# Two hybrid layers reordered: convolution columns first, delta-net operands during the projection, attention units between the matmuls of the inverse's levels

## The chip, the cores and the metric

One core of one Trainium2 chip runs the kernel; the time is device microseconds, before the change 1755.29 us in the median of three runs (1745.7 to 1759.51). All work is float32. A matrix product of the projections is made as three matmuls of the numbers' high and low halves, the others as float32 matmuls, which the trace records as two instructions each.

## What is computed

Two hybrid layers, then two layers of another kind, which the change leaves alone. 256 tokens, width 1024. A hybrid layer projects the normalised input, runs three mixers on the columns and projects their joined outputs back; a gated feed-forward block follows.

```python
h = rms_norm(x, norm_mix) * (1 + sc_m) + sh_m
(aq, ak, av, bq, bkc, bvc, bks, bvs, bkw, bvw, bg, cqkv, cz, ca, cb) = jnp.split(h @ w_in, points, axis=-1)
o_a = banded_attention(apply_rope(aq), apply_rope(ak), av, A_WINDOW, attn_sinks)
o_b = nsa_mixer(bq, bkc, bvc, bks, bvs, bkw, bvw, bg, ...)   # compressed, selected, windowed: three gated softmaxes
o_c = gated_delta_net(cqkv, ca, cb, cz, conv_w, A_log, dt_bias, gdn_norm)
x = x + gt_m * (jnp.concatenate([o_a, o_b, o_c], axis=-1) @ w_out)
```

The third mixer:

```python
q, k, v = split(silu(short_causal_conv(cqkv, conv_w)))       # width 4, one channel at a time
q = l2norm(q) * dk ** -0.5; k = l2norm(k)
beta = sigmoid(b); g = -exp(A_log) * softplus(a + dt_bias)
decay = exp(gc_i - gc_j) for j <= i                          # gc: running sum of g in a chunk
a_mat = strictly lower part of (k beta) k^T * decay
u, w = solve (I + a_mat) [v beta, k beta exp(gc)]            # the inverse
```

then a scan over the chunks with the state, and a gated norm with `silu(cz)`. `mod = silu(c) @ ada_w + ada_b` gives the shifts, scales and gates; its matrix is as wide as six widths, and its chunks of 512 columns are spread over the layer.

## The kernel before: how a hybrid layer is staged

Five engines run programs of their own, in order, tied by semaphores. Constants: `P` 128, `S` 256, `CH` 512, `SLOTS` 3, `AHEAD` 3, `LEVELS` 7, `DEPTH` 3.

**Weights.** SP loads chunks of 512 columns (2 MB) into `ring`, which has three slots: the load of chunk n waits for the end of chunk n-3 (`load`), which is the last matmul of a projection chunk, or for an `ada` chunk ACT's copy of its sums (`acc_ready`). Each chunk is two halves. For each half ACT makes the high part (`high`, L1253; three buffers, so a half waits for the use of the half three before it), DVE the low part (`low`, L1676), and PE runs the 48 matmuls of a half (`three`, L623 to L625). ACT issues `high(u+3)` after it has taken the two tiles of half u out of PSUM (`take`, L1270), in its program order: what stands behind a `high` on ACT waits for that chunk's DMA too. The same holds for DVE and `low`.

**Order of chunks in a hybrid layer.** Five column chunks: two for the attention inputs (`raw` tiles 0 to 7, of which 0 to 5 get the rotary embedding), three for the convolution (12 tiles); then `cz`; then `w_tok` (276 columns, 1.1 MB: values, gates, a, b). An `ada` chunk stands behind the third and the fifth.

**Input stage.** PE runs the chunks; `rotate(j)` puts the rotation matmul of a raw tile (L971) between column tiles, and DVE's three operations of it (L1965 to L1967) come back to PE as `rope_done`. DVE runs the convolution: per group of four tiles four operations of the first tap (L1995) and twelve of the others (L1997); ACT the silu (L1385).

**Preparation.** `token_major` (L785): 24 transposes to token-major form, copied by ACT (L1306); `log_decays` (L799, L801); the compression MLP (L1006, L1015, L1022, L1024).

**Attention.** Eight units a layer (two of mixer A, three for each query half of mixer B), with keys of width 128, 256, 15, 128, 128, 15, 256, 256. A unit is a chain over four engines: `scores` on PE (L738), `logits` on DVE (bias and maximum, L1705, L1708), `exps` on ACT (L1276), `recip` on DVE (L1721, L1724), the multiplication on POOL (L2192), `transposes` on PE (L748), `copy_pt` on ACT (L1287), `values` on PE (L761), at the end of an output `evac` on DVE (L1733). Scores alternate between banks 0 and 1 and banks 2 and 3, transposes use 4 and 5, so three units are in flight. DVE makes the delta-net operands in seven steps between units (L1805 to L1828).

**Delta net.** Seven `group`s of four transposes (L785), the products of keys (L820), their masks, and then seven levels of the inverse: T1 (L836, eight products of 128x128), ACT copies them (L1351), two updates (L844, L846), DVE subtracts them (L1858, L1860), POOL masks the matrix for the next level (L2232). PE issues `ada_dots` and `modulations` in levels 1 and 3. Then the tail: U and w, the state, the outputs, the gated norm, two groups of transposes; then the output projection.

`attention` and `delta_net` follow each other in all programs: the first level starts when the last unit is done.

Of the kernel before, what the change touches and what calls it, by code (L numbers as in the profile page):

```python
# [6 lines left out]
ALU = mybir.AluOpType  # L7
# [4 lines left out]
P = 128  # L12
# [31 lines left out]
KQ_BANKS = (4, 5, 6, 3)  # L44
# [16 lines left out]
CN_FIRST, V1_FIRST = 162, 64  # L61
# [20 lines left out]
def hybrid_then_mixture(nc, xT, c, vec1, vec2, consts, dist, table, ada, w_mix, w_tok, w_cmp, w_out, w_gu, w_dn,  # L82
# [46 lines left out]
    IN_ADA = (2, 4)  # L129
# [22 lines left out]

    def ada_bank(m):

        i = m % ADA_L
        return i + 2 if i < ADA_FIRST else 2 if i == ADA_FIRST + 2 else 6
# [12 lines left out]
    with ctx:  # L169
# [79 lines left out]
        tok = view(6656, 3, NCH, GD)  # L249
# [3 lines left out]
        Dm = view(10240, NCH, P)  # L253
        MT = view(21056, NCH, P)
        QKT = view(1024, NCH, P)
        MbT = view(13312, 2, NCH, P)
        X = view(15360, NCH, P)
# [66 lines left out]
        rows_ready = sem("rows_ready")  # L324
        mod_ready = sem("mod_ready")
# [84 lines left out]
        def stage(name, us, woven=False):  # L410

            stages[name] = (len(units), len(units) + len(us))
            for i, U in enumerate(us):
# [3 lines left out]
                U["bank"] = 2 if woven else 2 * ((len(units) + i) % 2)  # L417
# [80 lines left out]
        def _(sp):  # L498
# [35 lines left out]
            for l in range(L1):  # L534
# [11 lines left out]
                for j, at in enumerate(phases[f"in{l}"]["at"]):  # L546
# [5 lines left out]
                    if j in IN_ADA:  # L552
                        load_ada(m + IN_ADA.index(j))
                load(phases[f"tok{l}"]["n0"], w_tok[l], KT * TOKW)
                load_phase(f"cmp{l}", w_cmp[l], 0, full)
# [38 lines left out]
        def _(pe):  # L594
# [4 lines left out]
            def tile_free(name, j):  # L599

                t0 = phases[name]["t0"]
                if name.startswith("tok"):
# [64 lines left out]
            def columns_chunk(name, nn, j, src, ready=None, after=None):  # L667

                for part in range(2):
# [7 lines left out]
                    for m in range(2):  # L677
                        t = j + 2 * part + m
                        tile_free(name, t)
                        channel_tile(bank[:, t % 4, 0:S], w, m * P, src).then_inc(gemm_ready, 1)  # L680
                        if after:
                            after(t)

            def tokens_chunk(name, nn, j):

                for part in range(2):
# [3 lines left out]
                    for qt in range(QT):  # L690
                        if part == 0:
                            tile_free(name, j + qt)
                        last = token_tile(bank[:, (j + qt) % 4, CH // 2 * part:CH // 2 * (part + 1)], w, 0, CH // 2,
# [13 lines left out]
            def ada_dots(m):  # L707
# [3 lines left out]
                for k in range(KT):  # L711
                    rows = slice(32 * (k % 4), 32 * (k % 4) + 32)
                    last = nc.tensor.matmul(bank[rows, ada_bank(m), :], c_wide[:, k, :], w[:, k, :],
                                            start=k < 4, stop=k >= 4, tile_position=(0, 32 * (k % 4)))
                last.then_inc(rows_ready, 1)
# [1666 lines left out]
```

## Time and profile before

| | us |
|---|---|
| median of three runs | 1755.29 |
| the profiled execution, its own time | 1758.94 |
| its span, first to last instruction | 1757.1 |
| PE busy in the span | 1564.1 (89%) |
| DVE / ACT / POOL busy | 1031.5 / 785.3 / 273.1 |
| mean granted clock of PE | 0.934 |
| layer 0, first matmul of the input to first of the output projection | 43.1 to 273.2 |
| layer 1, the same | 534.5 to 758.0 |

Columns of a view of stretches: busy microseconds of an engine and its count of instructions, then the granted PE clock (1.00 is 2.4 GHz, 0.50 is 1.2 GHz), the DMA share and GB/s. In the chain of waits a row has start, length and what the time went into. "Idle before" in square brackets is what an instruction's engine waited for.

### The profile page before, as it was taken

The numbers are of one execution on the slowest core, as the hardware profiler recorded it, in microseconds if no ns is written. First come the engines' busy times: TensorE is split into PE (matmuls) and PEld (weight loads), VectorE is DVE, ScalarE is ACT, GpSimd is POOL, SyncE is SP. The second block draws the span as 40 slices with busy tenths as digits, with TensorE's granted clock in tenths as the row PEclk, the third lists the DMA queues.
The fourth block names the chain that finished last, engine by engine and source line by source line (L and its number), as shares of the span: only waits on it lengthen the run. The fifth ranks groups of instructions, "written<-read, shape, count | busy, mean of one in ns | idle before, by whom it ended". The sixth has DMA issues, their size and how long they took to land.

```text
span 1757.1 us, 29189 instructions
## 1 busy us (share of the span) xinstructions
PE 1564.1 (89%) x12266; PEld 1470.0 (84%) x12266; DVE 1031.5 (59%) x1324; ACT 785.3 (45%) x1178; POOL 273.1 (16%) x102
## 2 busy tenths in 40 slices
PE   5899798989898986989999899569999999999997
PEld 2886487989898864879999799448999988889997
DVE  1575536795664765367554533685876454478743
ACT  3335423434234354334533444354664355556642
POOL 0000255570530002554000000220000001100000
PEclk8997798999999988999999899679999999999999
DMA  8358324554453470244445734203553543245442
GB/s 362 145 218 314 122 97 165 205 205 176 180 195 144 180 285 41 97 152 157 176 156 180 258 144 158 96 1 101 187 191 133 198 172 133 98 154 175 161 151 88
DMA packets 30190, 287.82 MB, mean 164 GB/s; under 512 B 2887, under 2 KB 11367, under 8 KB 11784
## 3 DMA queue, kind: packets, MB, share of 16 engines
q1 hardware_dynamic: 28888, 269.51, 41.9%
q0 software_dynamic: 1152, 16.78, 2.4%
q8 instruction: 79, 1.29, 0.3%
q14 instruction: 23, 0.19, 0.0%
q10 hardware_dynamic: 48, 0.05, 0.0%
HBM read 285.23 MB, written 7.39 MB: 167 GB/s over the span
## 4 chain that ended last, share of the span: by engine, by line
PE 72%; DVE 16%; ACT 4%; issue 4%; DMA 3%; POOL 1%; SPq 0%; DVEq 0%; ACTq 0%
PE bank L623 20%; PE bank L624 19%; PE bank L625 19%; DVE w_lo L1676 4%; DMA ring<-w_mix 3%; PE bank L703 2%; DVE arena L1997 2%; ACT w_hi L1253 1%; PE bank L846 1%; PE bank L748 1%; PE bank L836 1%; DVE h L2118 1%; PE bank L844 1%; PE bank L738 1%; PE bank L761 1%
## 5 line engine op out<-in xcount | busy, mean ns | idle before, releaser
L623 PE MATMUL bank<-hi_T,w_hi 128*128 128x256 f32 x2248 | 653.3, 291 | 41.3 <-DVE h_lo L1659 16.4
L1676 DVE TENSOR_TENSOR w_lo<-ring,w_hi 128x2048 fp32r<-128x2048 f32 (+2 forms) x218 | 515.2, 2373 | 229.7 <-ACT w_hi L1253 228.0
L625 PE MATMUL bank<-hi_T,w_lo 128*128 128x256 f32 x2248 | 647.3, 288 | 0.0
L624 PE MATMUL bank<-h_lo,w_hi 128*128 128x256 f32 x2056 | 592.0, 288 | 0.0
L1253 ACT ACTIVATE w_hi<-ring 128x2048 fp32r<-128x2048 f32 (+3 forms) x226 | 391.8, 1735 | 349.6 <-PE bank L625 278.5
L623 PEld LDWEIGHTS bank<-hi_T,w_hi 128*128 128x128 f32 x2248 | 444.1, 198 | 47.7 <-issue 34.8
L625 PEld LDWEIGHTS bank<-hi_T,w_lo 128*128 128x128 f32 x2248 | 443.7, 197 | 0.0
L624 PEld LDWEIGHTS bank<-h_lo,w_hi 128*128 128x128 f32 x2056 | 405.8, 197 | 0.3
L623 PE MATMUL bank<-act_hi,w_hi 128*128 128x256 f32 x704 | 201.3, 286 | 11.7 <-DVE act_lo L1695 9.9
L624 PE MATMUL bank<-act_lo,w_hi 128*128 128x256 f32 x704 | 200.4, 285 | 0.0
L625 PE MATMUL bank<-act_hi,w_lo 128*128 128x256 f32 x704 | 200.3, 284 | 0.0
L623 PEld LDWEIGHTS bank<-act_hi,w_hi 128*128 128x128 f32 x704 | 135.8, 193 | 12.5 <-DVE act_lo L1695 10.5
L624 PEld LDWEIGHTS bank<-act_lo,w_hi 128*128 128x128 f32 x704 | 135.8, 193 | 0.0
L625 PEld LDWEIGHTS bank<-act_hi,w_lo 128*128 128x128 f32 x704 | 135.7, 193 | 0.0
L1270 ACT ACTIVATE arena<-bank 128x256 f32<-128x256 f32 (+3 forms) x99 | 39.1, 405 | 151.1 <-PE bank L625 151.1
L2155 DVE SCALAR_TENSOR_TENSOR arena<-bank,v,arena 128x254 f32<-128x254 f32 (+1 forms) x176 | 72.7, 475 | 37.2 <-ACT arena L1612 37.0
L2192 POOL TENSOR_TENSOR lg<-lg,rec 128x512 f32<-128x512 f32 (+2 forms) x24 | 31.2, 1301 | 398.8 <-DVE rec L1721 366.0
L2203 POOL TENSOR_TENSOR w_lo<-ring,w_hi 128x2048 fp32r<-128x2048 f32 x8 | 36.0, 4523 | 299.1 <-ACT w_hi L1253 299.1
L2212 POOL TENSOR_TENSOR arena<-arena 128x2048 f32<-128x2048 f32 (+1 forms) x16 | 80.0, 4999 | 1.3
L623 PE MATMUL bank<-w_hi,hi_T 128*128 128x256 f32 (+2 forms) x240 | 68.4, 285 | 8.7 <-DVE w_lo L1676 7.2
L624 PE MATMUL bank<-mix_lo,w_hi 128*128 128x256 f32 x256 | 74.5, 291 | 0.0
L2210 POOL TENSOR_TENSOR arena<-arena,c_silu 128x4096 f32<-128x4096 f32 x8 | 59.4, 7424 | 72.0 <-DMA arena<-ada 72.0
(234 smaller groups left out, 2014.6 us busy)
## 6 DMA issues: line engine op xcount, KB each, us to landing
ring<-w_gu SPq DMA_DIRECT2D x22, 2048.0 KB, 8.4
ring<-w_dn SPq DMA_DIRECT2D x32, 1408.0 KB, 6.0
ring<-w_up SPq DMA_DIRECT2D x22, 2048.0 KB, 8.1
ring<-ada SPq DMA_DIRECT2D x16, 2048.0 KB, 8.2
ring<-w_mix SPq DMA_DIRECT2D x12, 2048.0 KB, 8.2
arena<-ada POOLq DMA_DIRECT2D x8, 2048.0 KB, 9.5
ring<-even_in SPq DMA_DIRECT2D x8, 2048.0 KB, 8.3
ring<-odd_in SPq DMA_DIRECT2D x6, 2048.0 KB, 8.3
```

The costliest lines, as they stand in the source:

```text
L623: nc.tensor.matmul(out, wh, xh, start=start, stop=False)
L624: nc.tensor.matmul(out, wh, xl, start=False, stop=False)
L625: return nc.tensor.matmul(out, wl, xh, start=False, stop=stop)
L703: last = nc.tensor.matmul(bank[:, 7, 0:S], const("ones"), h[:, k, :], start=(k == 0), stop=(k == KT - 1))
L1253: nc.scalar.activation(w_hi[:, u % AHEAD, 0:size], ring[:, slot, part * size:(part + 1) * size], ACT.Copy)\
L1270: nc.scalar.activation(dst, src, func).then_inc(gemm_freed, 1)
L1676: V.tensor_tensor(w_lo[:, n % SLOTS, at], ring[:, n % SLOTS, at], w_hi[:, u % AHEAD, 0:size].bitcast(F32), ALU.subtract).then_inc(w_lo_rea ...
L1997: ins = V.scalar_tensor_tensor(out=conv[:, t, :], in0=src, scalar=wt, in1=conv[:, t, :], op0=ALU.mult, op1=ALU.add)
L2155: V.scalar_tensor_tensor(out=cv[:, b, half, shift:S], in0=bank[:, 2 * b + half, 0:S - shift], scalar=cw[:, tap, at], in1=cv[:, b, half, sh ...
L2203: G.tensor_tensor(w_lo[:, n % SLOTS, at], ring[:, n % SLOTS, at], w_hi[:, u % AHEAD, 0:size].bitcast(F32), ALU.subtract).then_inc(w_lo_rea ...
L2210: ch(G.tensor_tensor(ada_late, ada_late, along(c_silu, CH), ALU.mult))
L2212: ch(G.tensor_tensor(ada_late[:, 0:half], ada_late[:, 0:half], ada_late[:, half:2 * half], ALU.add))
```

## The change

The order of the chunks: the three convolution chunks (`conv{l}`), an `ada` chunk, `w_tok`, the two chunks of raw tiles, an `ada` chunk, `cz` (`in{l}`). The host packs the columns in that order.

In the input stage: ACT takes a convolution tile twice, once as it is and once scaled by the first tap, so DVE's first-tap operations go (12 a layer). The transposes to token-major form are issued between the chunks (`token_major(l, part)`), ACT takes the squared norms of q and k (16 activations with a sum) and scales v by beta (8) straight from PSUM, `log_decays` goes before `cz`, and all operands of the delta net (`unit_rows`, `decayed`) are made by DVE before the mixers start. `rotate` is now issued by hand for two tiles at a time, and waits for DVE's `rope_done` two tiles back.

In the mixers: `attention` and `delta_net` become one `mixing`. Scores and transposes of a unit both use banks 4 and 5 (`bank` 4); so `scores(u)` waits for `logits(u-1)` and for `copy_pt(u-2)`, and `transposes(u)` waits for `logits(u+1)`, the last scores that were issued. In level lv PE issues T1, an `ada` chunk's modulations and the first half of its dots (levels 1 to 5 and 1 to 4), the transposes of unit lv, the updates, the values of unit lv, the other half of the dots, the scores of unit lv+2. Unit 7 stands in the tail. `MbT` and `X` lie in `h` and `mix`; `ada` dots are made in halves of 256 columns through bank 7. ACT's high halves for the output projection move to levels 5 and 6 and the tail, POOL's low halves behind unit 7.

```diff
-        phase(f"in{l}", ["columns"] * 5 + ["tokens"], ada_after=IN_ADA)
+        phase(f"conv{l}", ["columns"] * 3, ada_after=(2,))
         phase(f"tok{l}", ["rows"], KT * TOKW // 2)
+        phase(f"in{l}", ["columns"] * 2 + ["tokens"], ada_after=(1,))
```

PE, in `scores`, then the input stage and the levels:

```diff
+                elif U["bank"] == 4:
...
+                    if u:
+                        pe.wait_ge(logits_done, u)
+                    if u - first >= 2:
+                        pe.wait_ge(pt_ready, u - 1)
...
+            def input_columns(l, ready):
+                columns_chunk(conv_name, 0, 0, src, ready)
+                columns_chunk(conv_name, 1, 4, src)
+                columns_chunk(conv_name, 2, 8, src, parts=(0,))
...
+                token_major(l, 0)
+                columns_chunk(conv_name, 2, 8, src, parts=(1,))
+                ada_dots(m)
...
+                token_major(l, 1)
+                columns_chunk(name, 0, 0, src, first_bank=2, parts=(0,))
+                modulations(m, m + 1)
+                token_major(l, 2)
+                columns_chunk(name, 0, 0, src, first_bank=2, parts=(1,))
+                rotate(l, 0)
+                rotate(l, 1)
+                columns_chunk(name, 1, 4, src, first_bank=2, parts=(0,))
+                rotate(l, 2)
+                rotate(l, 3)
+                columns_chunk(name, 1, 4, src, first_bank=2, parts=(1,))
+                ada_dots(m + 1)
+                log_decays(l)
+                tokens_chunk(name, 2, 8, 2, parts=(0,))
+                rotate(l, 4)
+                rotate(l, 5)
+                tokens_chunk(name, 2, 8, 2, parts=(1,))
+                modulations(m + 1, m + 2)
...
                 for lv in range(LEVELS):
-                    if lv == 3:
-                        modulations(m_next, m_next + 1)
                     pe.wait_ge(mb_ready, l * LEVELS + lv + 1)
-                    if lv in (1, 3):
-                        ada_dots(m_next + lv // 2)
...
                         last.then_inc(t1_ready, 1)
+                    if 2 <= lv <= 5:
+                        modulations(m + lv, m + lv + 1)
+                    if 1 <= lv <= 4:
+                        half_dots(m + 1 + lv, 0)
+                    transposes(u0 + lv)
...
                         last.then_inc(dx_ready, 1)
+                    if lv == 0:
+                        pe.wait_ge(kc_ready, l + 1)
+                    values(u0 + lv)
+                    if 1 <= lv <= 4:
+                        half_dots(m + 1 + lv, 1)
+                    if lv + 2 < len(range(*stages[f"hybrid{l}"])):
+                        scores(u0 + lv + 2)
```

ACT, in the input stage, and DVE, at the end of a level:

```diff
+                conv_silu(l, 0)
+                conv_half(4)
+                rows_of(l, 0)
+                conv_half(5)
+                conv_silu(l, 1)
+                ada_rows(m)
+                high(u0 + 6 + AHEAD)
...
+                high(u0 + 7 + AHEAD)
+                rows_of(l, 1)
+                conv_silu(l, 2)
+                raw_half(0)
...
+                    recip(u0 + lv + 1)
+                    evac(u0 + lv)
+                    if lv + 2 < len(range(*stages[f"hybrid{l}"])):
+                        logits(u0 + lv + 2)
```

The order of the loads on SP's queue, from the second chunk of layer 0's projection, before:

```order
L506 DMA ring<-w_mix 128x4096 x2
L506 DMA ring<-ada 128x4096
L506 DMA ring<-w_mix 128x4096 x2
L506 DMA ring<-ada 128x4096
L506 DMA ring<-w_mix 128x4096
L506 DMA ring<-w_tok 128x2208
L506 DMA ring<-w_cmp 128x4096 x2
L506 DMA ring<-ada 128x4096 x4
```

and now:

```order
L511 DMA ring<-w_mix 128x4096 x2
L511 DMA ring<-ada 128x4096
L511 DMA ring<-w_tok 128x2208
L511 DMA ring<-w_mix 128x4096 x2
L511 DMA ring<-ada 128x4096
L511 DMA ring<-w_mix 128x4096
L511 DMA ring<-w_cmp 128x4096 x2
L511 DMA ring<-ada 128x4096 x4
```

The half-sized `w_tok` now stands behind the first `ada` chunk, and only it lies between that and the next full chunk.

ACT's program behind the take of the last two convolution tiles, now (L1308 is `high`, L1522 the silu, L1320 `ada_rows`, L1384 and L1386 `rows_of`, L1333 `take`):

```order
L1308 ACTIVATE w_hi<-ring 128x2048
L1522 ACTIVATE arena<-arena 128x1024
L1320 ACTIVATE arena<-bank 128x512
L1308 ACTIVATE w_hi<-ring 128x2048
L1333 ACTIVATE arena<-bank 128x276 x2
L1423 ACT_TABLE_LOAD
L1423 ACTIVATE small<-arena 128x12
L1424 ACTIVATE small<-arena 128x4
```

and the stretch of before with the second silu and the first `w_tok` halves (L1253 is `high`, L1385 the silu, L1265 `ada_rows`, L1270 `take`):

```order
L1270 ACTIVATE arena<-bank 128x256 x2
L1253 ACTIVATE w_hi<-ring 128x1104
L1265 ACTIVATE arena<-bank 128x512
L1385 ACTIVATE arena<-arena 128x1024
L1253 ACTIVATE w_hi<-ring 128x1104
L1270 ACTIVATE arena<-bank 128x512 x2
```

Before, nothing that PE needs stood behind the silu's `high`; now the silu that PE's transposes wait for, and the copy of the `ada` sums that frees a ring slot, stand behind the `high` of a chunk that was loaded late.

ACT in levels 1 to 3, before (L1351 copies T1, L1265 `ada_rows`):

```order
L1351 ACTIVATE arena<-bank 128x512 x2
L1265 ACTIVATE arena<-bank 128x512
L1351 ACTIVATE arena<-bank 128x512 x4
L1265 ACTIVATE arena<-bank 128x512
L1351 ACTIVATE arena<-bank 128x512 x6
```

and now, from level 1 on (L1481 copies T1, L1327 is an `ada` half, L1350 `copy_pt`, L1339 `exps`):

```order
L1481 ACTIVATE arena<-bank 128x512 x2
L1327 ACTIVATE arena<-bank 128x256
L1350 ACTIVATE pT<-bank 128x512 x2
L1327 ACTIVATE arena<-bank 128x256
L1339 ACTIVATE lg,sums<-lg,negm 128x15 x4
L1481 ACTIVATE arena<-bank 128x512 x2
L1327 ACTIVATE arena<-bank 128x256
L1350 ACTIVATE pT<-bank 15x512
L1327 ACTIVATE arena<-bank 128x256
```

The exponentials of the next unit stand behind the second half of the `ada` dots, which PE makes at the end of a level.

## Rows read from the trace of the kernel before

**Rows 1.** The page: the chain that ended last, share of the span by engine

```profile
PE 72%; DVE 16%; ACT 4%; issue 4%; DMA 3%; POOL 1%; SPq 0%; DVEq 0%; ACTq 0%
```

**Rows 2.** Stretches: layer 0 whole, its attention; then layer 1 stage by stage

```profile
43.10:273.20 230.10, 197.01 (x1470) 169.50 (x1470) 124.81 (x230) 96.39 (x203) 38.10 (x20) 0.88 0.47 172
158.40:203.50 45.10, 35.01 (x189) 21.64 (x189) 26.91 (x50) 23.22 (x85) 12.67 (x11) 0.61 0.73 250
534.40:630.80 96.40, 88.36 (x685) 84.17 (x686) 58.91 (x101) 35.43 (x48) 0.00 (x0) 0.95 0.44 165
630.80:648.40 17.60, 15.09 (x149) 10.66 (x148) 9.99 (x28) 9.69 (x22) 0.00 (x0) 0.90 0.85 323
648.40:689.60 41.20, 28.85 (x189) 16.84 (x188) 27.10 (x50) 23.65 (x85) 12.68 (x11) 0.75 0.30 118
689.60:701.20 11.60, 8.66 (x45) 7.69 (x45) 5.47 (x10) 4.82 (x9) 0.00 (x1) 0.85 0.00 1
701.20:742.50 41.30, 38.59 (x328) 34.56 (x328) 16.73 (x26) 13.60 (x17) 19.82 (x8) 1.00 0.29 103
742.50:758.00 15.50, 9.94 (x80) 9.09 (x80) 4.59 (x14) 7.41 (x25) 5.60 (x2) 1.00 0.00 1
```

**Rows 3.** The chain that ended last, layer 1 (start, us, what)

```profile
534.47 0.55 PE bank L623
560.14 7.68 DMA ring<-w_mix
567.84 1.92 ACT w_hi L1253
...
605.60 2.20 DVE w_lo L1676
630.51 1.28 ACT L1439
...
732.64 1.16 PE bank L836 x8
738.75 1.16 PE bank L836 x8
758.05 0.38 PE bank L623
```

**Rows 4.** SP's issues of loads in layer 1, in order of time

```profile
548.62 0.33 SPq L506 DMA_DIRECT2D ring<-ada  x1
...
578.41 0.33 SPq L506 DMA_DIRECT2D ring<-w_mix  x1
```

**Rows 5.** DMA issues: KB each, median us to landing

```profile
bias_wide<-bias_dram SPq DMA_DIRECT2D x1, 6144.0 KB, 33.2
ring<-w_tok SPq DMA_DIRECT2D x2, 1104.0 KB, 5.0
```

**Rows 6.** The stretch behind a wait of 3.75 us in layer 1's input stage

```profile
574.00:578.00 4.00, 4.00 (x24) 4.00 (x23) 3.81 (x5) 0.00 (x0) 0.00 (x0) 0.58 0.00 0
```

**Rows 7.** Groups by form in layer 1's mixing and input (busy us, mean ns)

```profile
L2203 POOL TENSOR_TENSOR w_lo<-ring,w_hi 128x2048 fp32r<-128x2048 f32 x3 | 13.5, 4518 | 0.0
L2192 POOL TENSOR_TENSOR lg<-lg,rec 128x1024 f32<-128x1024 f32 x3 | 6.1, 2019 | 5.7 <-DVE rec L1724 3.8 <-DVE rec L1721 1.8
L1276 ACT ACTIVATE lg<-lg,negm 128x256 f32<-128x256 f32 x12 | 5.9, 497 | 0.9 <-DVE negm L1708 0.7 <-DVE esink L1713 0.2
L1705 DVE SCALAR_TENSOR_TENSOR lg<-bank,cn 128x1024 f32<-128x1024 f32 x3 | 3.7, 1224 | 1.5 <-PE bank L738 1.5
L1385 ACT ACTIVATE arena<-arena 128x1024 f32<-128x1024 f32 x3 | 3.2, 1053 | 3.0 <-DVE arena L1997 3.0
```

**Rows 8.** PE in attention at full clock: eight transposes

```profile
658.90 1.10 PE L748 MATMUL bank<-cn,lg 128*128 128x128 f32 x8 [0.17 <-POOL lg L2192]
```

**Rows 9.** DVE and POOL in order of time, layer 0's attention

```profile
191.12 1.52 DVE L1724 TENSOR_TENSOR rec<-rec,small 128x4 f32<-128x4 f32 x1
190.36 4.26 POOL L2192 TENSOR_TENSOR lg<-lg,rec 128x1024 f32<-128x1024 f32 x2 [3.78 <-DVE rec L1724]
```

More of the change, by code:

```diff
@@ L59 @@
 CNW = 2782
-CN_FIRST, V1_FIRST = 162, 64
+CN_FIRST, V1_FIRST = 162, 112
 class Chain:
@@ L665, in token_tile, with columns_chunk @@
                 return last
-            def columns_chunk(name, nn, j, src, ready=None, after=None):
-                for part in range(2):
+            def columns_chunk(name, nn, j, src, ready=None, first_bank=0, parts=(0, 1)):
+                for part in parts:
                     u = phases[name]["u0"] + 2 * nn + part
@@ L679, in columns_chunk, with tokens_chunk @@
                         tile_free(name, t)
[L680 to L686, printed above, removed]
+                        channel_tile(bank[:, (first_bank + t) % 4, 0:S], w, m * P, src).then_inc(gemm_ready, 1)
+            def tokens_chunk(name, nn, j, first_bank=0, parts=(0, 1)):
+                for part in parts:
                     u = phases[name]["u0"] + 2 * nn + part
@@ new lines, in mixing @@
+            def mixing(l):
+                m = ADA_L * l + ADA_FIRST
+                u0 = stages[f"hybrid{l}"][0]
+                pe.wait_ge(xpe_ready, 2 * (l + 1))
+                for kv in range(2):
+                    nn = phases[f"cmp{l}"]["n0"] + kv
+                    chunk_in(nn)
+                    w = ring[:, nn % SLOTS, :].rearrange("p (k n) -> p k n", k=CMP_PAIRS)
+                    for k in range(CMP_PAIRS):
+                        rows = slice(32 * (k % 4), 32 * (k % 4) + 32)
+                        last = nc.tensor.matmul(bank[rows, 6, S * kv:S * kv + S], xpe[:, kv, k, :], w[:, k, :],
+                                                start=k < 4, stop=k >= CMP_PAIRS - 4, tile_position=(0, 32 * (k % 4)))
+                    last.then_inc(gemm_ready, 1)
+                pe.wait_ge(rope_done, 7 * (l + 1))
+                scores(u0)
+                pe.wait_ge(gemm_freed, phases[f"out{l}"]["t0"])
@@ new lines, in blocks @@
+            def blocks(l):
+                ch(V.memset(xpe[:, :, :, :], 0.0))
+                dve.wait_ge(gemm_freed, phases[f"in{l}"]["t0"] + 8)
+                for kv, pe_name in enumerate(("pe_k", "pe_v")):
+                    for two, rows in enumerate((LO, HI)):
+                        base = raw[rows, 6 + kv, :].rearrange("p (n q a) -> p a q n", q=8, a=2)[:, two]
+                        for hf in range(2):
+                            last = V.tensor_tensor(
+                                xpe[rows, kv, 8 * hf:8 * hf + 8, 0:N_CMP], base[:, :, hf:hf + N_CMP],
+                                along(vec(l, pe_name)[rows, 8 * hf:8 * hf + 8], N_CMP), ALU.add)
+                    last.then_inc(xpe_ready, 1)
@@ L2006, in _ @@
-                dve.wait_ge(gate_exp, l + 1)
-                ch(V.tensor_scalar(small[:, 0:32], small[:, 0:32], 1.0, None, ALU.add))
-                ch(V.reciprocal(small[:, 0:32], small[:, 0:32]))
-                softplus(l)
-                decays(l)
-                attention(f"hybrid{l}", operands(l))
-                delta_net(l)
+                input_columns(l)
+                mixing(l)
                 dve.wait_ge(mod_ready, m + 6)
```

625 lines of the change are left out of this document (327 added, 298 removed).

## Prediction

> **What bounds the kernel now.** I read the page's chain first: 72% of it is PE, 16% DVE [rows 1]. Then the stretches of the two layers that are touched. A hybrid layer takes 230.1 us in layer 0 and 223.6 (534.4 to 758.0) in layer 1 [rows 2]; the remaining 1303 us of the span have no changed instruction. In layer 1 PE is busy 88.4 of 96.4 us in the input stage and 38.6 of 41.3 in the levels, at clocks 0.95 and 1.00. In attention it is busy 28.9 of 41.2 at clock 0.75, in layer 0 35.0 of 45.1 at 0.61, so even the busy part is stretched [rows 2]. The time to win is there: a unit is a chain over four engines, and no dense work of PE lies beside it. The chain of waits and SP's issues give the input stage's pace: chunks end at 548.62, 560.14 and 578.41 [rows 3, 4].
>
> **Input stage, layer 1, clock zero at its first matmul (534.47 [rows 3]).** A full chunk takes 560.14-548.62 = 11.5 us, a half 5.8; the first chunk 14.15 (clock) [rows 3, 4]. A load lands after 7.7 us [rows 3], `w_tok` after 5.0 [rows 5]; then ACT's high half 1.9, DVE's low half 2.2 [rows 3]; a table load 1.28 [rows 3], a silu 1.05 [rows 7]. The new order puts these in series four times:
> - `w_tok` may load when chunk 2 ends, 25.7; landed 30.7; its `high` (1.1, half the size) stands ahead of the first silu on ACT: silu done 34.1. PE is done with the half ahead of the transposes at 31.5. **Idle 2.6.**
> - The first raw chunk loads at the end of the third chunk, 40.8, landed 48.5. ACT's `high` 50.3, then silu 2 at 51.4. PE had `ada` dots (1.9) and `w_tok` (6.2), done 48.9. **Idle 2.5.** Transposes, then raw half 1 from 52.5 to 58.3.
> - The second raw chunk waits for the copy of the `ada` sums, behind that silu: 52.0, landed 59.7. ACT stands at its `high` until 61.6, then norms of eight tiles (3.1, from 0.25 to 0.6 each), table and silu: 67.1. PE was ready at 59.2. **Idle 7.9.**
> - `cz` loads at the end of the first raw chunk, 75.5, landed 83.2, high 85.0, low 87.2. DVE's `low` stands ahead of the first rotary tile, for which PE waits from 82.2 until 88.4, and 1.2 for the next. **Idle 7.4.**
>
> A wait of 3.75 us was followed by clock 0.58 for 4 us [rows 6], where 4.0 us of matmuls did the work of 2.3: I add 1.7 behind each of the two long ones, 3.4. PE's own work: before 88.4 busy, of which some 1.5 was such slow clock, so 86.9; plus 24 transposes at 1.10/8 = 0.14 [rows 8], 3, and `log_decays` 1.9. That is 91.8. Sum 91.8+2.6+2.5+7.9+7.4+3.4 = 115.6 against 96.4: **+19**. DVE's 12 first taps (0.3 each) and ACT's 12 added takes lie beside PE and change nothing; ACT's waits are loads, not work. The price is the series of load, high, silu, and with two of three slots behind an `ada` chunk and `w_tok` PE has only 8 us of work to cover a load's 12.
>
> **Mixing, layer 1.** Before, from 630.8 to 758.0: 127.2 us. PE's work in it at full clock: each stretch's busy time by its clock, 15.1 x 0.90 + 28.9 x 0.75 + 8.7 x 0.85 + 38.6 + 9.9 = 91.2 [rows 2]; less the 4.9 that moved to the input: 86.3. What of the rest stays:
> - the key products wait for copies, the masks for the products: 11.6-8.7 = 2.9 stays [rows 2];
> - the tail is a chain of small steps: 15.5-9.9 = 5.6 stays [rows 2];
> - in a level, a unit's steps: with width 256 logits 2 x 1.22+0.3 = 2.7, exps 4 x 0.5 = 2.0, POOL 2.0 [rows 7], `recip` 0.35, copy 1.1: 8.2 off PE. PE has in a level the 5.4 of T1 and updates (of a period of 738.75-732.64 = 6.1 [rows 3]), the dots 1.9, modulations 0.8 and 2 to 3 of the unit: 10 to 11 in levels 1 to 4. That covers the 8.2. It doesn't where the shared banks make `transposes(u)` wait for `logits(u+1)`: level 0 (1.3), level 1 (0.5), levels 5 and 6 without dots (1.4 and 1.1). Sum 4.3.
>
> 86.3+2.9+5.6+4.3 = 99. This takes full clock for all; the levels had it with 93% busy [rows 2]. So layer 1: 115.6+99 = 214.6 against 223.6, **-9**. Scaling a whole stretch by its mean clock overstates the work, since the slow part of the stretch is where the busy rows are: eight transposes took 1.10 at full clock [rows 8], and counted piece by piece attention is 19 and not 21.7, the small pieces of the other stretches about 2 less. I take 95 for the mixing: layer 1 at 210.6, **-13**.
>
> **Layer 0** does the same work: 210.6, plus one thing of its own. The 6 MB `bias_wide` transfer takes 33.2 us [rows 5]; it is issued behind the fourth `ada` load, which now waits for level 1, near 189 us, so it ends near 223, and the first output chunk lands near 228 behind it. ACT's `high` for it stands in level 5, near 225: 2 to 3 us. 213 against 230.1: **-17**.
>
> Late parts: POOL's three low halves (4.5 each [rows 7]) now start in the tail, 14 us before the output projection; the first is needed at its start and the others 5.8 and 11.6 later: hidden, 4 if the tail were 10 shorter. The feed-forward stage starts as before.
>
> **Sum**: 1758.94-30 = 1729 for the profiled execution's own time. The median shown is 3.65 below that time, so 1755.3-30 = 1725; since two of the three bounds I chose (full clock in the mixing, no wait inside levels 2 to 4) are on the good side I take **1728**.
>
> **Bounds.** If the four series of the input stage were fully hidden, the input would be 92+2 and the gain 2 x 20 larger: 1688. If the clock falls in the mixing as in attention before (0.75 for a third of it), 8 a layer are lost: 1744.
>
> **Rivals.**
> 1. *The loads are hidden after all* (another engine's order lets ACT pass): for it, only 8 of 96 us were idle before [rows 2], with three slots too; against it, the silus stand behind the `high` in ACT's program. 1690.
> 2. *DVE and POOL hold each other up.* A `recip` product of 128x4 took 1.52 us instead of 0.16, beginning while POOL's 2.3 us multiplication ran and ending with it [rows 9]. In the levels POOL has 2.0 of mask and up to 2.0 of unit in each, and DVE's small product stands on the way to the next unit. My order of events has POOL done before DVE's product in each level; if it is wrong in each, 2.0 x 7 x 2 = 28 come back: 1756, no change. The Trainium skill (SBUF — State Buffer, "Who interferes with whom") says that a VectorE operation with two SBUF inputs and a GpSimd operation that reads SBUF exclude each other for the whole instruction; by that rule, which those two rows agree with, it depends only on which starts first.
> 3. *The units serialise: slower.* Banks 4 and 5 serve scores and transposes of all units, so fewer are in flight. A unit alone is 8.2 off PE plus 2.9 on it, 11 for width 256 (three), some 6.3 for 128 (three), 4.6 for 15 (two): 61 us. If nothing of it lies beside the 41.3 of the levels, that pair costs 102 where I count about 64: +38 a layer, 1804. It decides from 15 us of uncovered chain a layer on. For it: ACT's `exps` stand behind the second half of the dots, so each unit's chain starts at a level's end. Against: a level of 10 us is longer than the 8.2. Half of it gives 1766, all 1804: I name 1785.
>
> **How the numbers follow.** A measurement of this kernel tells 1% (17.6 us) from no change. The forecast's own case, 1710 to 1737, has 0.5; rival 1 0.12; rival 2 and a fallen clock, 1738 to 1772, 0.26; rival 3 0.12. Faster by over 1% (under 1737.7): 0.62; within 1% 0.26; slower 0.12. Leaving out half of rival 1 and rival 3 gives a range of 1696 to 1763.
>
> **What would show it.** In the changed trace: the input stage to `cz`'s last matmul at 115 us from its start, with PE idle twice for over 6 us, ended by ACT's silu and DVE's rope tile; the chain there with three `w_mix` loads a layer. Levels 1 to 4 at 10 to 11 us each, 5 near 9.5; granted clock 1.00 in the levels; mixing 95 to 99. `bias_wide` issued near 189. Wrong would be: levels over 13 us with PE waiting for POOL (rival 3 or 2), or an input stage under 100 (rival 1).

## The result, and the profile after

| | before | changed |
|---|---|---|
| median, us (20 executions each) | 1753.3 (1742.33 to 1761.31) | 1742.86 (1732.74 to 1748.69) |
| ratio, 95% interval | 1 | 0.9938 (0.9919 to 0.9956) |
| first profiled execution: own time, span, clock | 1758.94, 1757.1, 0.934 | 1732.74, 1731.0, 0.944 |
| layer 0 / layer 1 in it | 230.1 / 223.6 | 217.6 / 217.7 |
| layer 0 / layer 1, mean of three profiles | 227.1 / 223.6 | 217.5 / 218.6 |
| page, chain: PE / DVE | 72% / 16% | 75% / 11% |

The change gains 10 us, 0.6%, where 27 from the shown median (30 from the profiled execution) were forecast. The time lies among those that the forecast gave to rival 2 and a fallen clock (1738 to 1772). The two first profiles lie 26 us apart since that of before was one of its slower executions and that of the change its fastest, so every stage below is read in more than one profile.

Stretches of the changed kernel (columns as in [rows 2]): layer 0; the unchanged feed-forward stage behind it; layer 1 whole, its input stage, its preparation, its levels, its tail; the rest:

```profile
43.40:261.00 217.60, 185.97 (x1534) 165.25 (x1534) 117.06 (x212) 109.53 (x260) 37.55 (x20) 0.91 0.49 182
261.00:512.60 251.60, 234.31 (x1857) 230.90 (x1857) 179.55 (x119) 101.10 (x100) 124.04 (x30) 0.97 0.55 205
512.60:730.30 217.70, 183.78 (x1535) 164.14 (x1535) 114.79 (x211) 107.61 (x258) 37.56 (x20) 0.93 0.37 141
512.60:630.10 117.50, 97.12 (x730) 92.20 (x734) 67.55 (x121) 59.04 (x120) 0.00 (x0) 0.90 0.36 136
630.10:650.70 20.60, 17.94 (x177) 14.29 (x176) 11.80 (x23) 9.59 (x29) 5.38 (x3) 0.99 0.75 307
650.70:709.20 58.50, 56.85 (x547) 47.69 (x547) 25.23 (x49) 25.93 (x80) 16.85 (x13) 0.98 0.40 145
709.20:730.30 21.10, 11.87 (x91) 9.95 (x89) 10.22 (x18) 13.06 (x32) 15.33 (x4) 0.88 0.00 0
730.30:1731.00 1000.70, 916.08 (x7354) 892.64 (x7354) 597.63 (x739) 479.39 (x655) 79.26 (x28) 0.96 0.41 150
```

Against [rows 2]: the input stage went from 96.4 to 117.5 us, everything behind it from 127.2 to 100.2. Attention's 41.2 and the levels' 41.3 us, 82.5 together, are now 58.5 with PE busy for 56.9 of them at clock 0.98. Mixing works as meant; the tail, 15.5 us before, is now 21.1 with 11.9 busy.

The starts of T1 in levels 1 to 5 of layer 1, PE in order of time:

```profile
662.35 2.05 PE L945 MATMUL bank<-mix,h 128*128 128x128 f32 x16
...
672.45 2.05 PE L945 MATMUL bank<-mix,h 128*128 128x128 f32 x16
...
682.52 2.05 PE L945 MATMUL bank<-mix,h 128*128 128x128 f32 x16
...
693.10 2.05 PE L945 MATMUL bank<-mix,h 128*128 128x128 f32 x16
...
702.68 2.05 PE L945 MATMUL bank<-mix,h 128*128 128x128 f32 x16
```

Levels 1 to 3 take 10.1 to 10.6 us and level 4 takes 9.6. PE's idle spells over 0.5 us in the levels are one of 1.0 in level 4, whose cause the profile doesn't show, and one of 0.65 for POOL in level 5. Where PE does wait in the input stage (the forecast's four series), in order of time:

```profile
546.18 1.10 PE L813 MATMUL bank<-cn,arena 128*128 128x128 f32 x8 [3.06 <-ACT arena L1522]
...
565.21 1.97 PE L813 MATMUL bank<-cn,arena 128*128 128x128 f32 x8 [4.02 <-ACT arena L1522]
...
580.57 1.76 PE L813 MATMUL bank<-cn,arena 128*128 128x128 f32 x7 [6.35 <-ACT arena L1522]
...
603.03 2.45 PE L831 MATMUL bank<-arena,cn 128*128 128x256 f32 x4 [6.89 <-DVE arena L1922]
```

Forecast were 2.6, 2.5, 7.9 and 7.4. In the tail: PE's wait for the second half of the gated norm, DVE ahead of it (L1781 makes the low part of the attention half of `mix`), POOL beside it (L2324, the three low halves):

```profile
727.72 1.12 PE L813 MATMUL bank<-cn,arena 128*128 128x128 f32 x4 [5.55 <-DVE arena L2044]
...
720.33 1.13 DVE L2044 SCALAR_TENSOR_TENSOR arena<-bank,small,arena 128x128 f32<-128x128 f32 x4
721.37 5.04 DVE L1781 TENSOR_TENSOR mix_lo<-mix,hi_T 128x1024 fp32r<-128x1024 f32 x1
...
726.53 1.13 DVE L2044 SCALAR_TENSOR_TENSOR arena<-bank,small,arena 128x128 f32<-128x128 f32 x4
...
711.85 13.48 POOL L2324 TENSOR_TENSOR w_lo<-ring,w_hi 128x2048 fp32r<-128x2048 f32 x3
```

POOL's three products of 4.5 us run from 711.85 to 725.33, so the third begins near 720.84. DVE's product begins 0.5 us later and ends 1.1 us after it. Whether those 5.04 us are 1.2 us of work behind a lock is the first thing tested.

### The profile page after: what moved, and what is told of

Read it like the earlier page. It is cut to its first block, busy times and chain, and to the rows that moved or that the text cites. A ratio compares the mean times of both kernels' runs of the same rounds, so it can differ in the third digit from the quotient of the medians.

```text
span 1731.0 us, 29521 instructions
## 1 busy us (share of the span) xinstructions
PE 1544.2 (89%) x12394; PEld 1463.3 (85%) x12394; DVE 1015.2 (59%) x1288; ACT 811.4 (47%) x1292; POOL 278.6 (16%) x102
## 4 chain that ended last, share of the span: by engine, by line
PE 75%; DVE 11%; DMA 5%; ACT 5%; issue 3%; POOL 0%; SPq 0%; DVEq 0%; ACTq 0%
PE bank L631 21%; PE bank L632 20%; PE bank L633 20%; DMA ring<-w_mix 4%; DVE w_lo L1775 3%; PE bank L709 2%; PE bank L945 2%; ACT w_hi L1308 2%; PE bank L962 1%; PE bank L789 1%; PE bank L776 1%; DVE h L2236 1%; PE bank L960 1%; PE bank L733 1%; PE bank L764 1%
## 5 line engine op out<-in xcount | busy, mean ns | idle before, releaser
L631 PE MATMUL bank<-hi_T,w_hi 128*128 128x256 f32 x2248 | 653.2, 291 | 37.7 <-DVE h_lo L1758 16.4
L1308 ACT ACTIVATE w_hi<-ring 128x2048 fp32r<-128x2048 f32 (+2 forms) x226 | 392.0, 1735 | 331.0 <-PE bank L633 281.6
L631 PEld LDWEIGHTS bank<-hi_T,w_hi 128*128 128x128 f32 x2248 | 444.4, 198 | 43.4 <-issue 33.1
L631 PE MATMUL bank<-act_hi,w_hi 128*128 128x256 f32 x704 | 200.7, 285 | 10.4 <-DVE act_lo L1794 8.9
L631 PEld LDWEIGHTS bank<-act_hi,w_hi 128*128 128x128 f32 x704 | 135.8, 193 | 11.2 <-DVE act_lo L1794 9.6
L1333 ACT ACTIVATE arena<-bank 128x256 f32<-128x256 f32 (+3 forms) x75 | 29.9, 410 | 122.6 <-PE bank L633 122.6
L2324 POOL TENSOR_TENSOR w_lo<-ring,w_hi 128x2048 fp32r<-128x2048 f32 x8 | 36.0, 4526 | 299.4 <-ACT w_hi L1308 299.4
L2331 POOL TENSOR_TENSOR arena<-arena,c_silu 128x4096 f32<-128x4096 f32 x8 | 65.8, 8223 | 70.9 <-DMA arena<-ada 70.9
L631 PE MATMUL bank<-w_hi,hi_T 128*128 128x256 f32 (+2 forms) x240 | 69.4, 289 | 0.0
L633 PE MATMUL bank<-w_hi,h_lo 128*128 128x256 f32 (+2 forms) x240 | 68.5, 285 | 0.0
```

The lines of the kernel that those rows point to most:

```text
L631: nc.tensor.matmul(out, wh, xh, start=start, stop=False)
L633: return nc.tensor.matmul(out, wl, xh, start=False, stop=stop)
L1308: nc.scalar.activation(w_hi[:, u % AHEAD, 0:size], ring[:, slot, part * size:(part + 1) * size], ACT.Copy)\
L1333: nc.scalar.activation(dst, src, func).then_inc(gemm_freed, 1)
L2324: G.tensor_tensor(w_lo[:, n % SLOTS, at], ring[:, n % SLOTS, at], w_hi[:, u % AHEAD, 0:size].bitcast(F32), ALU.subtract).then_inc(w_lo_rea ...
L2331: ch(G.tensor_tensor(ada_late, ada_late, along(c_silu, CH), ALU.mult))
```

## The experiments

In each, stage lengths run from the first matmul of a layer's input (L631) to the first of its output projection. Medians of runs from one series are compared with each other, and the ratio is to the kernel before in the same series.

### Base: the changed kernel again

> The changed kernel once more, unaltered, with its own profile, as the base for the others of this series. The first profile of it was its fastest run (span 1731.0, clock 0.944) and the profile of before one of the slower (1757.1, 0.934). Theory: layers 0 and 1 repeat within 1.5 us each (217.6 and 217.7 from the first matmul of the convolution columns to the first of the output projection), and what differs between runs lies in the 1296 us of unchanged stages. Rival: the two layers themselves scatter by 5 us or more with the clock, and the single profiles can't be compared stage by stage.

1740.41 us, ratio 0.9933 (0.9904 to 0.9961). Its stretches, as above:

```profile
43.80:260.90 217.10, 184.38 (x1535) 164.58 (x1535) 116.96 (x212) 109.65 (x260) 37.55 (x20) 0.92 0.49 182
260.90:520.10 259.20, 237.00 (x1856) 234.09 (x1856) 181.04 (x119) 101.23 (x100) 119.89 (x30) 0.95 0.53 199
520.10:738.80 218.70, 185.55 (x1535) 165.66 (x1535) 114.92 (x211) 107.76 (x259) 37.56 (x20) 0.91 0.37 141
```

The layers repeat within 1 us; the feed-forward stage, with no changed instruction, takes 259.2 instead of 251.6.

### The tail: POOL's third low half later

```diff
                 for u in range(phases[f"out{l}"]["u0"], phases[f"out{l}"]["u0"] + AHEAD):
+                    if u == phases[f"out{l}"]["u0"] + AHEAD - 1:
+                        pool.wait_ge(mix_ready, 3 * l + 1)
                     low(u)
```

> POOL starts the third low half for the output projection only after DVE has made the low part of the attention half of the mix. In the changed kernel that product of 128x1024 took 5.04 us, begun 0.53 us behind POOL's third low half and ended with it, where the same form takes 1.22 us elsewhere, and PE stood idle for 5.55 us for it. Theory (the two engines exclude each other on SBUF): the product takes 1.2 us, the wait of PE goes from 5.55 to 1.8 us, and each layer is 3.8 us shorter, 7.5 in all: ratio to before about 0.990. POOL's third half ends 1.7 us later, 11 us before PE wants it. Rival: the norm of the second chunk or ACT's last high parts are late instead and PE waits as long; the time stays.

1729.13 us, 11.3 under the base; ratio 0.9878 (0.984 to 0.9917). DVE, POOL and PE in layer 1's tail, in order of time:

```profile
729.20 1.22 DVE L1781 TENSOR_TENSOR mix_lo<-mix,hi_T 128x1024 fp32r<-128x1024 f32 x1
...
730.50 4.54 POOL L2324 TENSOR_TENSOR w_lo<-ring,w_hi 128x2048 fp32r<-128x2048 f32 x1 [1.79 <-DVE mix_lo L1781]
...
731.72 0.66 PE L813 MATMUL bank<-cn,arena 128*128 128x128 f32 x4 [1.72 <-DVE arena L2044]
```

The same product takes 1.22 us and PE waits 1.72 instead of 5.55, 3.8 less. The layers are 3.7 and 3.0 us shorter than in the base (213.4 and 215.7). So 3 to 4 us a layer of the tail were DVE standing still for POOL. The median moved by 11.3, more than the 6.7 of the two layers; the intervals of the two ratios (0.9904 to 0.9961 and 0.984 to 0.9917) allow that much.

### The input stage: ACT's order

```diff
-                conv_half(5)
-                conv_silu(l, 1)
-                ada_rows(m)
+                take_conv(l, 10)
+                take_conv(l, 11)
+                conv_silu(l, 1)
+                ada_rows(m)
+                high(u0 + 5 + AHEAD)
```

The first silu goes ahead of `w_tok`'s first `high` in the same way, and `high(u0 + 7 + AHEAD)`, `rows_of(l, 1)` and the third silu ahead of the gates' exponentials.

> In the input stage only ACT's order is altered: each silu of the convolution and the copy of the ada sums stand ahead of the high half of a chunk that is still being loaded, and the exponentials of the gates behind the third silu. Theory (the waits are the series of load, high, silu, and the late copy of the sums holds back the next load by 10 us): PE's waits of 3.06 and 4.02 us for the first two silus go to under 1, the third of 6.35 to about 3, the second raw chunk loads near 43 us from the stage's start instead of 53; the wait for the rotary tile stays near 6.9, since DVE still stands at the low half of cz. Input stage 117.5 to about 107; the whole kernel 20 us shorter than the changed one. Rival (the loads themselves are the bound, two of three slots being taken): the chunks land no earlier, PE waits for the high half instead of the silu, gain under 5 us in all.

1720.83 us, 19.6 under the base; ratio 0.9825 (0.9789 to 0.9861). SP's issues in layer 1 of the changed kernel, then of this one:

```profile
553.06 12.93 SPq L511 DMA_DIRECT2D ring<-w_mix  x2
```

```profile
547.77 2.84 SPq L511 DMA_DIRECT2D ring<-w_mix  x2
```

The second of the two raw chunks was issued 12.6 us behind the first (at 565.66), and is now 2.5 behind it: 39.7 us from the stage's start instead of 53.1. Layer 0's input stage is 105.6 us against 116.8 in the base, layer 1's 107.0, as expected. No idle spell of PE over 0.2 us is ended by a silu any more; PE waits for a load's high and low half instead, in layer 1:

```profile
561.27 0.58 PE L631 MATMUL bank<-hi_T,w_hi 128*128 128x256 f32 x1 [4.49 <-DVE w_lo L1780]
```

This wait (3.13 in layer 0) is the part of the rival that is true: the first raw chunk can't load before the third chunk ends. The rotary wait stayed (6.66 and 7.27).

### The input stage: DVE's order

```diff
-                lows(12, 13)
                 rope(l, 0)
                 rope(l, 1)
+                lows(12, 13)
                 lows(13, 14)
```

> In the input stage only DVE's order is altered: the first two rotary tiles ahead of the low half of cz. Theory: the 6.89 us (layer 1) and 6.53 us (layer 0) for which PE waits for a rotary tile go, 13.4 in all; PE then meets the log decays and cz itself: cz is loaded at 589.6 and landed at 597.5, PE wants it near 604 in place of 615, so little comes back. Ratio to before about 0.986. Rival (the wait only moves to cz's load and its halves, or to the compression weights behind it): no change of time beyond 2 us.

1722.46 us, 17.9 under the base; ratio 0.9829 (0.9791 to 0.9867). The whole wait was a loss: the layers are 208.4 and 210.6, 8.7 and 8.1 us shorter than in the base, where PE had waited 6.3 and 7.3 for this tile. The gain is larger than the 13.4 expected: in layer 1's input stage PE's idle time fell by 6.5 us and its busy time by 1.5. What is left of it, in layer 1, is a wait for the fourth rotary tile at the log decays:

```profile
606.54 0.36 PE L838 MATMUL bank<-small,cn 128*128 128x8 f32 x2 [2.14 <-DVE arena L1922]
```

### All three

> The three alterations of tail, act and rope together. Alone they gave 11.3, 19.6 and 17.9 us against the unaltered changed kernel at 1740.4. Theory (independent waits on one path): they add up to 49 less what the scatter of the medians makes of them; counted in the traces, 3.7 + 9.9 + 8.5 a layer, 44 in all: 1693 to 1699, ratio 0.967 to 0.970. The input stage takes near 100 us, with PE waiting for nothing over 5 us. Rival (with the silus out of the way PE is early at the next load, cz or the compression weights, each 8 to 12 us behind a freed slot): half of the gain of act and rope comes back as waits for DMA, high and low: 1710 or more.

1696.17 us, ratio 0.9648 (0.9616 to 0.968): in time the theory's sum. Stretches: layer 0, its input stage, layer 1:

```profile
45.60:241.10 195.50, 181.40 (x1534) 162.15 (x1534) 113.13 (x212) 106.75 (x258) 36.37 (x20) 0.95 0.54 202
45.60:143.60 98.00, 93.67 (x729) 89.61 (x730) 69.78 (x122) 58.05 (x120) 0.00 (x0) 0.94 0.48 186
504.90:697.10 192.20, 176.42 (x1535) 157.66 (x1535) 110.98 (x211) 104.94 (x257) 36.45 (x20) 0.98 0.42 160
```

The input stage of layer 0 needs 98.0 us with 93.7 busy, where the changed kernel takes 115.9 and the kernel before 97.4. So 18 of the 18.5 us by which it had grown were the order of events on ACT and DVE, not the order of the loads. In layer 1 it is 97.5 us, against 117.5 and 96.4. PE's busy time in layer 1 fell too, from 185.6 to 176.4 at clock 0.98 instead of 0.91: the same matmuls, with fewer waits before them. PE's longest wait in the stage is 4.0 us, for a low half.

### The units taken out of the levels

In all four programs the loop over the levels is split in two, first the units, then the levels, and POOL waits for DVE's subtraction before it masks for the next level. On PE:

```diff
+                for lv in range(LEVELS):
+                    transposes(u0 + lv)
...
+                    values(u0 + lv)
+                    if lv + 2 < len(range(*stages[f"hybrid{l}"])):
+                        scores(u0 + lv + 2)
                 for lv in range(LEVELS):
```

> The one part of the change undone that was to bring the gain: the seven attention units run one after the other ahead of the seven levels, on the same two banks as in the changed kernel, in all four programs; the input stage and the tail are as in the changed kernel. Theory (the forecast's third rival as arithmetic: a unit alone is 11 us at width 256, 6.3 at 128, 4.6 at 15, so two, three and two of them 50 us; the levels alone 41, against the 60 that both take now): 31 us more a layer, 62 in all: 1803, ratio to before about 1.03. It shows what the levels hide. Rival (the units overlap by themselves on two banks, the chain of one beside the matmuls of the next): attention takes 30 to 40 us, and the loss is 10 to 20 a layer, 1760 to 1780.

1807.73 us, ratio 1.0289 (1.0245 to 1.0332). Seven units alone in layer 0, then the levels; then layer 1 whole:

```profile
178.00:225.70 47.70, 26.97 (x133) 16.51 (x133) 14.53 (x34) 16.75 (x68) 10.07 (x10) 0.53 0.03 13
225.70:282.30 56.60, 49.31 (x450) 42.97 (x448) 17.14 (x28) 13.73 (x22) 16.86 (x8) 0.92 0.75 259
561.50:807.60 246.10, 198.72 (x1535) 172.94 (x1535) 111.68 (x211) 108.03 (x259) 37.89 (x20) 0.84 0.32 125
```

The chain of units costs 47.7 us (50 by the forecast's prices), at clock 0.53, so PE's part runs near its lower level of 1.2 GHz. Interleaving on these two banks is worth 27 (246.1 against 218.7) to 38 us a layer (255.4 against 217.1), about the 31 expected, and no less than the 27 that the change gains behind the input stage. The levels did not fall back to 41 us as expected but to 56.6: they still carry `ada` dots in four levels, begin at a low clock, and PE waits 5.7 us in level 6 of layer 0 for a copy of T1 behind a `high`.

### The kernel before again

> The kernel before once more, unaltered, for a second profile. The forecast's sum was made against one profile (span 1757.1, clock 0.934) in which the two hybrid layers took 230.1 and 223.6 us. Theory (the base was read from a slow instance: attention of layer 0 ran at clock 0.61 and took 45.1 us, in layer 1 at 0.75 and 41.2): here the two layers take 3 to 8 us less in all, most of it in attention, at a higher clock there; with 435.7 us for the two layers in the second profile of the changed kernel the gain in them is then 10 to 15 us, near the 11.5 that the medians show. Rival: the layers repeat within 1 us, 453 to 454, the gain in them is 18, and 6 us are given back in unchanged stages.

1749.14 us. The stretches:

```profile
43.40:270.10 226.70, 190.49 (x1471) 165.17 (x1471) 124.92 (x230) 96.22 (x202) 38.14 (x20) 0.91 0.49 175
270.10:524.30 254.20, 235.81 (x1857) 232.51 (x1857) 180.61 (x118) 101.09 (x100) 122.98 (x30) 0.96 0.54 203
524.30:748.40 224.10, 190.34 (x1470) 163.16 (x1470) 122.75 (x229) 94.61 (x202) 38.13 (x20) 0.91 0.36 137
```

Layer 0 is 3.4 us shorter than in [rows 2], layer 1 no shorter: the gain in the layers is 15 against this profile, so a small part of the miss lies in the base. Most of the 3.4 is attention, as expected: from layer 0's first scores to its first product of keys it took 51.7 us at clock 0.61 in the first profile and 49.1 at 0.73 in this one. The feed-forward stage differs by 7 us between the kernel's own profiles (261.2 and 254.2), as in the changed kernel. DVE and POOL in it, at the third product for a late `ada` chunk (L2331), first in the first profile of the changed kernel, then in its second:

```profile
335.80 2.29 DVE L1775 TENSOR_TENSOR w_lo<-ring,w_hi 128x2048 fp32r<-128x2048 f32 x1 [1.42 <-ACT w_hi L1308]
...
336.19 8.78 POOL L2331 TENSOR_TENSOR arena<-arena,c_silu 128x4096 f32<-128x4096 f32 x1 [12.51 <-DMA arena<-ada]
```

```profile
335.77 8.53 DVE L1775 TENSOR_TENSOR w_lo<-ring,w_hi 128x2048 fp32r<-128x2048 f32 x1 [1.42 <-ACT w_hi L1308]
...
335.14 7.01 POOL L2331 TENSOR_TENSOR arena<-arena,c_silu 128x4096 f32<-128x4096 f32 x1 [11.49 <-DMA arena<-ada]
```

Whichever begins first runs its length and the other takes the rest of it on top. The Trainium skill (SBUF — State Buffer, "Who interferes with whom") says this of a VectorE operation with two SBUF inputs beside a GpSimd operation that reads SBUF; the rows agree. Which is first was decided here by tenths of a microsecond: DVE's product began at 335.80 and 335.77, and POOL's as soon as the DMA of its operand had landed, at 336.19 and 335.14.

### POOL's long product cut up

```diff
-                ch(G.tensor_tensor(ada_late, ada_late, along(c_silu, CH), ALU.mult))
+                for k in range(0, KT, 2):
+                    ch(G.tensor_tensor(ada_late[:, k:k + 2], ada_late[:, k:k + 2], along(c_silu[:, k:k + 2], CH), ALU.mult))
```

and the first sum in two pieces.

> The kernel before, with POOL's long product for a late ada chunk (128x4096, 7.0 us undisturbed) cut into four of 128x1024, and its first sum (128x2048) into two; nothing else. In the feed-forward stage behind layer 0 this product meets DVE's low half of 128x2048: where POOL began first (347.82 against 347.94 in the first profile) DVE's 2.29 us took 9.04, PE waited 4.8 and then 3.0 us and the stage took 261.3 us; where DVE began first (344.84 against 345.15 in the second) it took 2.29, and the stage 254.3. Theory (the median of a series is a mixture of the two orders, set by when a DMA lands): with short pieces DVE waits for at most 1.8 us, the stage takes 254 or less in every execution, the median falls to 1746 to 1749 and the executions lie closer together. Rival (the pieces hold DVE up as long in sum, only more often): the stage stays at 258 to 262 and the time at 1752 to 1757.

> The changed kernel with the same cut of POOL's product. Its own two profiles had both orders too: DVE first in one (feed-forward stage of layer 0 251.6 us), POOL first in the other (259.3). Theory: the change itself is worth what the two layers show, 15 to 18 us, and the 11 of the medians carry the mixture of this race; so the time here is 15 to 18 us under split_before, near 1731. Rival (part of the gain really comes back in the unchanged stages): 9 to 12 us under split_before.

1731.89 us for the kernel before (ratio 0.9873, 0.9836 to 0.991), 1716.83 for the changed one (0.9797, 0.9763 to 0.9831). Both gain about 24 us (by the ratios 22 and 25), some three times what the theory said for the kernel before: I had counted one collision, while the cut also shortens the others (POOL makes eight such products, six of them in this stage). The stage, in the two:

```profile
272.10:512.30 240.20, 230.98 (x1856) 229.01 (x1856) 155.44 (x119) 100.75 (x100) 142.56 (x54) 0.98 0.58 215
```

```profile
260.30:499.80 239.50, 230.76 (x1857) 228.97 (x1857) 157.09 (x119) 100.82 (x100) 141.38 (x54) 0.98 0.57 215
```

DVE's busy time, which holds its standing still, falls from between 180 and 183 us to 155 and 157, and the stage is shorter by 12 to 21. PE's idle time in it falls from 18.4 us in the second profile of the kernel before to 9.2, and its busy time from 235.8 to 231.0 at clock 0.98 instead of 0.96. One part of the theory failed: the executions don't lie closer together. The six of each span 14.8 and 12.8 us, where the eleven of the kernel before in this series span 16.6.

With the collisions cut short the change is worth 15.1 us by medians and 13.3 by the ratios, whose intervals (0.7% wide each) don't tell this from the 11 of the uncut kernels. The layers differ by 18.1 (453.2 against 435.1), the stretch behind layer 1 by 2.4 the other way (992.6 against 995.0).

> The three alterations of all3 (tail, act, rope) and the cut of POOL's product. all3 had 1696.2 us, with the feed-forward stage of layer 0 at 263.8 us and PE waits of 4.6 and 2.3 us in it. Theory: 7 to 9 us shorter, 1687 to 1690, ratio to before 0.960 to 0.963. Rival (the pieces cost as much as the collision): 1696.

All four alterations: **1670.15 us, ratio 0.9526 (0.9493 to 0.9558)**, faster than both kernels. Against all3 it is 26 us by medians and 21 by the ratios, not 7 to 9, for the same reason; the stage behind layer 0 is 241.3 us instead of 263.8.

### A third profile of each

> The kernel before once more, a third profile, for the order in which DVE and POOL begin in the feed-forward stage of layer 0. Theory: the layers take 450 to 454 us again, and the stage behind layer 0 is either near 254 (DVE's low half first) or near 261 (POOL's product first), nothing between; the time of the execution goes with it. Rival: the stage takes other lengths whatever the order, so that the scatter has another cause.

> The changed kernel once more, a third profile. Theory: the layers take 435 to 436 us again; the stage behind layer 0 is near 252 (DVE first) or near 259 (POOL first). With 15 to 18 us of gain in the layers and, by the two split kernels, 0 to 2.5 given back behind them, the ratio to before lies between 0.990 and 0.994. Rival: the ratio stays at 0.9935 or above with the stage in the shorter form, and the layers' gain is lost elsewhere.

Before: 1749.48 us; layers 224.6 and 223.2, and the stage behind layer 0 257.4 us. The layers' 447.8 us lie below the 450 to 454 expected. In the stage POOL was first at the third product (DVE's half took 8.67 us). At the fourth it was first too, but by 3.2 us, and DVE's half took 5.93 where it had taken 7.19, begun 2.0 behind POOL, in the first profile. What a collision costs goes by how far apart the two begin, so there are lengths between 254 and 261: that part of the theory was too simple. Changed: 1742.47 us, ratio 0.9938 (0.9916 to 0.9961); layers 217.7 and 219.4, 437.1 in all where 435 to 436 were expected; the stage 251.8, DVE first.

The rival's condition was met to the letter: the ratio stayed at 0.9938 with the stage in its short form. But this profile's span is 1728.5, and those of the two others of the changed kernel 1731.0 and 1736.9, where a median execution has one near 1741, so it doesn't say what the median one does. The three profiles of before (1757.1, 1747.3, 1747.7) average 1750.7, close to its median.

## Why the prediction was wrong

The time lay in the range and the sign was right, but the gain was 10 us and not 27 to 30. By its steps:

- **Input stage: right.** 115.6 forecast, 117.5 measured in layer 1 (115.9 in layer 0); the four idle spells came at the four places named. Their sum, 20.3 us against 20.4, is so near by luck: single spells are off by up to 1.6 us, and the sum is 17.7 in layer 0 and 19.3 in layer 1 of the second profile. `act` and `rope` showed that the series load, high, silu is the cause of three of them and the low half of `cz` ahead of the rotary tiles that of the fourth, and all3 that removing them gives 98 us. The bound put 40 us on the four series; `act` and `rope` alone gave 19.6 and 17.9.
- **Levels: right, with the waits counted too dear.** Levels 1 to 4 took 9.6 to 10.6 us, with no serial chain; DVE's `recip` product took 0.16 us in each of them, so POOL didn't hold it up. The sum had 4.3 us of waits in the levels; PE was idle for 1.7. `apart` showed what is hidden there: 27 to 38 us a layer.
- **Late parts: the step that failed most.** "POOL's three low halves now start in the tail ...: hidden." I asked only when PE needs them. They also hold up DVE's 1.2 us product, on the way to the last transposes. The sum had 5.6 us of waits in the tail; PE was idle for 9.2. `tail` took 3.8 us a layer off PE's wait, 7.6 in all, and 6.7 off the two layers. Rival 2 had the mechanism, but looked for it in the levels alone, at 2.0 us a time; the rows of [rows 9] spoke of any POOL product beside a DVE product, and the diff had just moved three of 4.5 us beside one. That `tail` then took 1729 us, the forecast's own number, is luck: the layers account for 6.7 of its 11.3.
- **"I take 95 for the mixing":** the sum said 99 and I lowered it by 4 for matmuls counted too dear. Measured were 100.2: PE busy 86.7, idle 13.5. The sum had 86.3 of work and 12.8 of waits, the lowered one 82.3. Each stretch's busy time by its clock (0.99, 0.98 and, in the tail, 0.88) gives 83.9 of work at full clock, so part of the correction had its place, but the clock wasn't full for all. That the sum of 99 came so near is luck too: 3.6 too little in the tail stand against 2.9 too much in the levels and the preparation.
- **Layer 0's own term** (213, with 2 to 3 us for a late `high`): 217.6, of it 3.8 the tail. `bias_wide` was issued at 193.9 (forecast near 189), but the wait didn't come: PE has no idle spell for a `high` in the levels, and the output projection's first matmul waits 1.4 us for DVE's `mix_lo`, as in the kernel before, and not for a load. Layer 0 took as long as layer 1 (217.7).
- **Sum.** Layers against the base profile: -5.9 and -12.5, so -18.4 instead of -30; 7.6 of the 11.7 missing are the tail (6.7 by the layers of `tail`), 1.9 the input of layer 1, and the rest of 2.2 is the sum of the terms above that missed either way.
- **The base.** The layers took 453.7 us in the profile that I used and 450.8 and 447.8 in two others, mean 450.8; the changed kernel's mean is 436.1 (435.3, 435.8, 437.1). So the layers gain 14.7, and of the 18.4 that the first profiles showed 2.9 were the luck of the base and 0.8 that of the changed kernel. Subtracting what was read in one long execution from the median of others was wrong by that much.
- **What stays open.** The layers gain 14.7 us, the medians 10.4 to 11.6, and the 3 to 4 us between them are not placed. The stretches without a changed instruction don't show them: behind layer 1 the three profiles of before take 998.9 to 999.3 us and those of the changed kernel 995.9 to 1000.7, mean 998.2, and the stage behind layer 0 takes 257.6 in the mean of before and 254.2 in that of the changed kernel. The 2.4 us given back behind layer 1 in the pair of cut kernels lie within that scatter. All three profiles of the changed kernel are shorter than a median execution of it, so where such a one is longer isn't known. It can also be noise: 14.7 us is just outside the interval of the first series (7.7 to 14.2) and inside that of the second (6.8 to 16.8).

Rival 1 (hidden loads) and rival 3 (serial units) didn't come, nor did a clock fallen to 0.75 in the levels: it was 0.98 in layer 1 and 0.95 in layer 0.

## What to carry to other kernels

When a change moves a long product on POOL, list each DVE product with two SBUF inputs that can now begin beside it, not only who needs POOL's result; cut long POOL products into pieces where DVE stands on the critical path. On an in-order engine put what others wait for ahead of an instruction that waits for a load: two reorderings of a few lines, `act` and `rope`, gave 19.6 and 17.9 us here, each more than the whole change. Read at least two profiles of the kernel before, and take a stage's price from their mean.

## What was not expected of the hardware

- A stage that the change leaves alone took 251.6 to 261.2 us in six profiles of the two kernels, and a race of two engines is part of it: a DVE product of 2.29 us takes 8.5 to 9.0 when POOL's 7.01 us product begins up to 0.6 us before it, and 2.29 when DVE begins just ahead. That the race makes the scatter of the whole time (8 us either way) isn't shown: with the product cut the executions spread about as widely.
- Cutting that product into four (and a sum into two) gave 24 us, 1.3% of the kernel, though POOL's busy time in the stage went up from between 120 and 124 us to 141 and 143.
- PE's granted clock was 0.53 over 47.7 us of short chains in which PE was busy for 27.0, and 0.95 over 59.5 us with the same units of the same layer between the levels' matmuls, where it was busy for 57.9 (in layer 1 0.98, with 56.9 of 58.5).
